# Stacked score matmuls, and PSUM banks taken by the planner's clocks

## The chip, the cores and the metric

The kernel runs on one core of a Trainium2 chip. The metric is the time of one execution on the device in microseconds (us). Three runs of the kernel before took 1472.0, 1473.97 and 1474.49 us; the median is 1473.97 us.

## The reference, cut to what matters

Two transformer-like blocks over 256 positions of width 1024, one after the other, all in float32. Four attentions lie in them, and the change is about their score matmuls:

```
# first block: an indexer picks 64 keys for each query, then 16 query heads over 4 key heads
logits = einsum('bqhd,bsd->bqhs', iqb, ik)            # 8 index heads of 64, one index key head
score  = einsum('bqhs,bqh->bqs', relu(logits), iwb)   # top 64 of it are the valid keys
att = einsum('bqgrd,bqkgd->bqgrk', qg, k_sel) * 64 ** -0.5   # 16 heads of 64, 4 key heads
p = softmax(where(valid, att, -inf)); o = einsum('bqgrk,bqkgd->bqgrd', p, v_sel)
# beside it in the first block: a gated recurrent layer (conv, two gates, scan) on 1024 channels
# second block, layer 0: differential attention, 4 heads with 2 maps of 64 each
sc = einsum('bqhmd,bshmd->bhmqs', q, k) * 64 ** -0.5; p = softmax(sc)
w = p[:, :, 0] - lam * p[:, :, 1]
# second block, layer 1: 8 query heads of 64 over 2 key heads, and beside it 8 heads of 96 (MLA)
```

Everything else is projections and five gated feed-forward layers (1024 to 2816 and back).

## The kernel before, in words

The 256 positions are two blocks of 128 rows. All big products (line 455) split each operand into a high and a low part and add three matmuls, `hi*hi`, `hi*lo`, `lo*hi`. Weights come in chunks of 128 x 1024 through six raw buffers; ScalarE copies a chunk to `WH` (line 403), VectorE subtracts to get `WL` (line 393), and TensorE runs through the chunks in order.

The program is written out by a planner in Python. Each engine has one queue in the order in which the planner emits, and a clock (`Q.at`) that an `Estimate` class advances by a guessed time for each instruction; `Q.when(token)` is the guessed end of an instruction. Big products are the main line. All else (attention units, the indexer called `chooser`, the recurrent steps `rnn`) are Python generators in a list `side`; `pump` steps those whose due time has come on TensorE's planned clock. In the fine stages a pump comes after every six matmuls of a 512-column product. Where the main line has to wait for a side branch, `onward` and `drain` step the branches alone and move TensorE's planned clock to the next due time.

PSUM has eight banks of 128 x 512 floats. `take` pops the bank that was given back longest ago; `give` puts a bank back with the token of its last reader. A taker emits its instruction at once, with a wait on that token: where the reader is late, TensorE stands in its queue and everything behind it stands too. `product` takes two banks, and before that steps branches until four are free.

An attention unit (function `one`, lines 576 to 679) handles two heads of one block of 128 queries. Its steps on TensorE: two transposes of a 128 x 64 query slice (line 586), copied to `QT` by ScalarE (line 587); two score matmuls (line 595), one for each head, whose weights are 64 x 128 (the head's 64 dimensions by 128 queries) and whose moving data are 64 x 128 or 64 x 256 of the turned keys `KT`; then softmax on VectorE and ScalarE (lines 609 to 625); transposes of the probabilities (line 650), copied to `PT` (line 654); products with the values (line 665), scaled into the output (line 671). Heads of 64 number 16 in the first block, 8 maps in layer 0 and 8 in layer 1, each for two query blocks, so 32 units have heads of 64; 8 units of MLA have heads of 96. Keys are turned by `turned_keys` (transposes at line 560, a ScalarE copy at line 563). The indexer does the same with 8 heads: transposes at line 1039, score matmuls at line 1052. A float32 matmul stands in the trace as two records, a transpose as one.

In layer 1 the keys of MLA are finished on VectorE (line 1583) before they are turned; layer 0 and layer 1 each end with a drained stretch, in which no product is left to cover the side branches.

Of the kernel before, what the change touches and what calls it, by code (L numbers as in the profile page):

```python
# [7 lines left out]
F32 = mybir.dt.float32  # L8
F32R = mybir.dt.float32r
# [49 lines left out]
class Estimate:  # L59
# [5 lines left out]
    def __init__(self):  # L65
        self.table = None

# [29 lines left out]
    def max(self, o, a):  # L97
        return 0.18 + 0.001 * width(a)
# [10 lines left out]
    def matmul(self, o, l, r, start=None, stop=None, skip_group_check=False):  # L109
        n = width(o)  # L110
        return max(0.108, 0.00045 * n) if l.dtype == F32R else max(0.215, 0.00177 * n)

    def transpose(self, o, i, ident):
        return 0.109
# [86 lines left out]
def build(nc, a, out):  # L201
    with ExitStack() as ctx:
        def sb(name, shape, dt=F32, c=ctx):
            return c.enter_context(nc.sbuf_tensor(name, shape, dt))
# [13 lines left out]
        SM = sb("SM", [128, 1024])  # L218
# [8 lines left out]
        with ExitStack() as c1:  # L227
# [14 lines left out]
            B1["T1"] = sb("T1a", [128, 320], F32, c1)  # L242
            B1["T2"] = sb("T1b", [128, 320], F32, c1)
        B2 = {}
        with ExitStack() as c1:
# [6 lines left out]
            B2["KT"] = sb("KT2", [128, 8, S], F32, c1)  # L252
# [8 lines left out]
        with ExitStack() as c1:  # L261
# [9 lines left out]
            B3["KG"] = sb("KG3", [128, 2, S], F32, c1)  # L271
# [21 lines left out]
        def program(plan):  # L293
# [7 lines left out]
            def small(n):  # L301
                i = pos["sm"]
                pos["sm"] += n
                assert pos["sm"] <= 1024
                return SM[:, i:i + n]
# [262 lines left out]

            def attention(units, d, dv, scale, PT, QT, slots, q, kt, v, kwaits, owaits, bias=None, lam=None, many=None, chosen=None, qs=None, sums=None, late=None, rings=None, first=0):
# [5 lines left out]
                def one(n, blk, hs, nk, o_ap):  # L575
# [4 lines left out]
                    qt = QT[0:d, n % nq, :]  # L580
# [63 lines left out]
                    held.add(("p", n % npt))  # L644
                    b, free = take()
# [12 lines left out]
                    while late is not None and not late:  # L658
                        yield
                    b, free = take()  # L660
# [220 lines left out]
            def rnn(p):  # L881
# [115 lines left out]
            IQT = B1["PT"][:, 0:2, :].rearrange("p a n -> p (a n)")  # L997
# [9 lines left out]
            def chooser():  # L1007
# [19 lines left out]
                ki = turned_keys(IKT, lambda b, h: QKI[:, b, 1792:1856], 1, 64, kr, bar)  # L1027
# [3 lines left out]
                for blk in range(2):  # L1031
                    yield
                    nk = 128 * (blk + 1)
                    kq = []
                    for h0 in (0, 4):
                        b, free = take()
                        for h in range(h0, h0 + 4):
                            j = (h - h0) * 128
                            tok = op("pe", lambda e, b=b, j=j, h=h, blk=blk: e.transpose(
                                PB[b][0:64, j:j + 128], heads[:, blk, 20 + h, :], ID[:, :]), free, kr)  # L1040
                        kq.append(op("act", lambda e, b=b, h0=h0: e.activation(
                            IQT[0:64, h0 * 128:h0 * 128 + 512], PB[b][0:64, :], ACT.Copy), tok, iq_free))
                        give(b, kq[-1])
                    kacc = None
                    for h in range(0, 8, 2):
# [29 lines left out]
                for h0 in (16, 0, 8):  # L1075
# [5 lines left out]
                kk = turned_keys(KT[:, :, :].rearrange("p h s -> p (h s)"),  # L1081
                                 lambda b, h: heads[:, b, 16 + h, :], 4, 64, kr2, bar)
# [4 lines left out]
                    units, 64, 64, 64 ** -0.5, B1["PT"], B1["QT"], [SR[:, i, :] for i in range(4)], lambda b, h: heads[:, b, h, :],  # L1087
                    lambda h: KT[:, h // 4, :], lambda kb, h: V1[:, kb, (h // 4) * 64:(h // 4) * 64 + 64],
# [161 lines left out]
            def layer0():  # L1250
# [5 lines left out]
                kws = Q.dma("pool", "d_ws", WS[:, :, :], a["ws"], bar)  # L1256
                rs_ = lambda: stage["rs"]
# [53 lines left out]
                def diff():  # L1311
                    while 0 not in turned_ or 1 not in turned_:
                        yield
                    yield turned_[1]
                    kk = turned_keys(KT[:, :, :].rearrange("p h s -> p (h s)"),
                                     lambda b, h: QK[:, b, 512 + h * 64:512 + h * 64 + 64], 8, 64, turned_[1], bar)
# [5 lines left out]
                        lambda b, h: QK[:, b, h * 64:h * 64 + 64], lambda h: KT[:, h, :],  # L1322
# [113 lines left out]
            def layer1():  # L1436
# [8 lines left out]
                gh = G[:, :, 0:640].rearrange("p b (h d) -> p b h d", d=64)  # L1445
# [29 lines left out]
                def gqa_heads(i, h0, h, name):  # L1475
# [8 lines left out]
                    ss, k = summed(SG[:, :, h0 * 64:(h0 + h) * 64], h, 64, kq)  # L1484
# [35 lines left out]
                def gqa():  # L1520
                    while "gk_n" not in flags:
                        yield
                    yield flags["gk_n"]
                    kk = turned_keys(KG[:, :, :].rearrange("p h s -> p (h s)"), lambda b, h: gh[:, b, 8 + h], 2, 64,
                                     flags["gk_n"], bar)
                    while "gq_n" not in flags:
# [7 lines left out]
                        units, 64, 64, None, B3["PT"], B3["QT"], rooms, lambda b, h: gh[:, b, h], lambda h: KG[:, h // 4, :],  # L1534
                        lambda kb, h: G[:, kb, 640 + (h // 4) * 64:640 + (h // 4) * 64 + 64],
# [86 lines left out]
                def evacuated(got_x, moves):  # L1622
# [8 lines left out]
                side.extend([gqa_heads(1, 8, 2, "gk"), gqa_heads(0, 0, 8, "gq"), gqa(), mla_shared(), mla_keys(),  # L1631
# [3 lines left out]
                    (lambda b: SG[:, b, 512:640], lambda p: p[:, 0:128], ACT.Square, rs_, rt_)))  # L1635
# [145 lines left out]
```

How the kernel before makes its waits and increments, by code:

```python
    def play(self, eng, e, sems):  # L173
        seen = {}
        for waits, fn, sem, n in self.q[eng]:
            need = {}
            for s, v in waits:
                if v > seen.get(s, 0):
                    need[s] = max(need.get(s, 0), v)
            for s, v in need.items():
                e.wait_ge(sems[s], v)
                seen[s] = v
            ins = fn(e)
            if n:
                ins.then_inc(sems[sem], n)
# [1508 lines left out]
        @block.sync  # L1694
        def _(e):
            Q.play("sp", e, sems)
            for s, v in final[0]:
                e.wait_ge(sems[s], v)
```

## Time and profile before

| what | value |
|---|---|
| median of three runs | 1473.97 us (1472.0 to 1474.49) |
| the profiled execution's own time | 1469.99 us |
| its span, first to last instruction | 1468.2 us |
| TensorE busy | 1418.3 us, 97% of the span, 7100 matmul records |
| VectorE busy | 881.9 us, 60% |
| ScalarE busy | 755.2 us, 51% |
| GpSimd busy | 10.6 us, 1% |
| DMA | 242.58 MB, 165 GB/s mean |
| mean granted TensorE clock | 0.986 of full speed |

The span ends at the last instruction; 1.8 us of the execution's time lie outside it. Busy shares are averages over stages: five feed-forward layers with nothing but big products, and three stages with attention in them (41 to 230 us, 698 to 772 us, 1172 to 1262 us). A matmul's record is longer than its share of the engine, because matmuls overlap: what one costs is read from the distance between starts.

### The profile page before, as it was taken

The page shows a single profiled execution, that of the slowest core. Times are in us where ns is not written, and L with a number is a line of the kernel's source. Part 1 is how long each engine was busy: PE and PEld are TensorE (multiplying, and loading weights), DVE is VectorE, ACT ScalarE, POOL GpSimd, SP SyncE. Part 2 cuts the span into 40 slices and gives each one's busy share as a digit, 9 for nine tenths or more (in the row PEclk, how much of TensorE's full clock was granted, in tenths as well). Part 3 has the DMA queues.
Part 4 walks back from the last instruction along what each step waited for, and adds up shares of the span by engine and source line. Part 5 has one row for each costly group of instructions (what it writes and reads, how often), then busy time and mean ns, then how long its engine had stood idle before and what let it go on. Part 6 is the DMA issues. An engine that isn't in the chain of part 4 may idle for free.

```text
span 1468.2 us, 18415 instructions
## 1 busy us (share of the span) xinstructions
PE 1418.3 (97%) x7100; PEld 1193.7 (81%) x7100; DVE 881.9 (60%) x1443; ACT 755.2 (51%) x1159; POOL 10.6 (1%) x18
## 2 busy tenths in 40 slices
PE   6999999899999999999979999999999979999999
PEld 6899887688887788888868888888888868888887
DVE  6878766655454645557876555555555684655553
ACT  5568754554443544445655544444444486554442
POOL 1000000000000000000000000000000000000000
PEclk9999999899999999999989999999999989999999
DMA  8544534465565465554525555655555440465561
GB/s 281 156 142 135 186 100 144 143 206 181 172 204 169 136 208 182 191 186 158 173 72 172 187 180 189 203 179 186 168 186 191 135 144 0 130 213 178 170 212 59
DMA packets 131768, 242.58 MB, mean 165 GB/s; under 512 B 8544, under 2 KB 21472, under 8 KB 131680
## 3 DMA queue, kind: packets, MB, share of 16 engines
q1 hardware_dynamic: 130768, 239.15, 50.7%
q0 software_dynamic: 624, 2.10, 0.5%
q8 instruction: 57, 0.93, 0.3%
q14 instruction: 31, 0.25, 0.1%
q10 hardware_dynamic: 288, 0.14, 0.0%
HBM read 240.31 MB, written 1.05 MB: 164 GB/s over the span
## 4 chain that ended last, share of the span: by engine, by line
PE 94%; DVE 3%; ACT 2%; DMA 0%; issue 0%; SPq 0%; DVEq 0%
PE PB L455 83%; PE PB L485 3%; PE PB L595 2%; PE PB L665 2%; PE PB L650 1%; PE PB L586 1%; PE PB L560 0%; PE PB L1052 0%; DMA X<-in_x_dram 0%; ACT SL L625 0%; DVE SM L530 0%; DVE SM L528 0%; DVE SM L529 0%; DVE WL L393 0%; PE PB L908 0%
## 5 line engine op out<-in xcount | busy, mean ns | idle before, releaser
L393 DVE TENSOR_TENSOR WL<-RAW,WH 128x1024 fp32r<-128x1024 f32 (+1 forms) x453 | 537.1, 1214 | 226.2 <-ACT WH L403 225.9
L403 ACT ACTIVATE WH<-RAW 128x1024 fp32r<-128x1024 f32 (+1 forms) x453 | 467.6, 1054 | 307.2 <-PE PB L455 304.2
L455 PE MATMUL PB<-WH,AT0h 128*128 128x512 f32 (+3 forms) x1328 | 505.0, 380 | 2.5 <-DVE AT0l L511 1.5
L455 PE MATMUL PB<-WH,AT0l 128*128 128x512 f32 (+3 forms) x1328 | 498.2, 375 | 0.0
L455 PE MATMUL PB<-WL,AT0h 128*128 128x512 f32 (+3 forms) x1328 | 498.2, 375 | 0.0
L455 PEld LDWEIGHTS PB<-WH,AT0h 128*128 128x128 f32 x1328 | 251.7, 190 | 47.3 <-ACT AT0h L506 2.2
L455 PEld LDWEIGHTS PB<-WH,AT0l 128*128 128x128 f32 x1328 | 251.3, 189 | 44.8
L455 PEld LDWEIGHTS PB<-WL,AT0h 128*128 128x128 f32 x1328 | 251.7, 190 | 42.2
L455 PE MATMUL PB<-WH,FTh 128*128 128x512 f32 x440 | 174.0, 395 | 0.0
L455 PE MATMUL PB<-WH,FTl 128*128 128x512 f32 x440 | 172.5, 392 | 0.0
L455 PE MATMUL PB<-WL,FTh 128*128 128x512 f32 x440 | 170.8, 388 | 0.0
L722 DVE SCALAR_TENSOR_TENSOR SR<-PB,SM,SR 128x512 f32<-128x512 f32 (+1 forms) x60 | 42.4, 706 | 136.0 <-PE PB L455 136.0
L455 PEld LDWEIGHTS PB<-WH,FTl 128*128 128x128 f32 x440 | 82.6, 188 | 19.3
L455 PEld LDWEIGHTS PB<-WL,FTh 128*128 128x128 f32 x440 | 82.6, 188 | 18.0
L455 PEld LDWEIGHTS PB<-WH,FTh 128*128 128x128 f32 x440 | 82.8, 188 | 16.0
L714 ACT ACTIVATE SR<-PB,SM 128x512 f32<-128x512 f32 (+1 forms) x60 | 39.3, 654 | 96.7 <-PE PB L455 93.8
L497 ACT ACTIVATE FTh<-PB 128x512 fp32r<-128x512 f32 x55 | 30.2, 596 | 103.2 <-PE PB L485 103.2
L500 DVE TENSOR_TENSOR FTl<-PB,FTh 128x512 fp32r<-128x512 f32 x55 | 35.7, 687 | 18.1 <-ACT FTh L497 18.1
L747 DVE SCALAR_TENSOR_TENSOR X<-PB,X 128x512 f32<-128x512 f32 x16 | 11.1, 692 | 49.6 <-PE PB L455 49.6
L455 PE MATMUL PB<-AT0h,WH 128*128 128x256 f32 x128 | 37.4, 292 | 0.0
L511 DVE SCALAR_TENSOR_TENSOR AT0l<-PB,CO,AT0h 128x256 fp32r<-128x256 f32 x64 | 26.7, 478 | 16.5 <-ACT AT0h L506 16.5
L455 PE MATMUL PB<-AT0l,WH 128*128 128x256 f32 x128 | 36.2, 283 | 0.0
(300 smaller groups left out, 1134.3 us busy)
## 6 DMA issues: line engine op xcount, KB each, us to landing
RAW<-in_ffn_w_gu_dram SPq DMA_DIRECT2D x88, 512.0 KB, 4.6
RAW<-in_ffn_w_gu_2b_dram SPq DMA_DIRECT2D x88, 512.0 KB, 4.5
RAW<-in_w_in_dram SPq DMA_DIRECT2D x48, 512.0 KB, 3.7
RAW<-in_ffn_w_down_dram SPq DMA_DIRECT2D x44, 512.0 KB, 4.2
RAW<-in_ffn_w_down_2b_dram SPq DMA_DIRECT2D x44, 512.0 KB, 4.1
RAW<-in_w_ffn_gate_dram SPq DMA_DIRECT2D x22, 512.0 KB, 4.5
RAW<-in_w_ffn_up_dram SPq DMA_DIRECT2D x22, 512.0 KB, 4.6
RAW<-in_w_ffn_down_dram SPq DMA_DIRECT2D x22, 512.0 KB, 4.6
```

The lines of the kernel that those rows point to most:

```text
L393: e.tensor_tensor(o, s, h, ALU.subtract), th, loaded[i], hl_free[i % NHL])
L403: th = op("act", lambda e, o=WH[i % NHL][:, 0:m], s=RAW[i % NRAW][:, 0:m]: e.activation(o, s, ACT.Copy), loaded[i], hl_free[i % NHL])
L455: e.matmul(o, l, r, start=s, stop=p, skip_group_check=feature_major)
L485: tok = op("pe", lambda e, o=o, s=src(blk, t): e.transpose(o, s, ID[:, :]), waits, free, ("d_id", 16))
L497: th = op("act", lambda e, o=hi, s=PB[b][:, 0:m]: e.activation(o, s, ACT.Copy), tok, dst.free)
L500: e.tensor_tensor(o, s, h, ALU.subtract), th, dst.free)
L511: e.scalar_tensor_tensor(o, s, g, h, ALU.mult, ALU.subtract),
L586: e.transpose(o, s, ID[:, :]), free, kwaits)
L595: e.matmul(o, qt[:, i * 128:i * 128 + 128], r, start=True, stop=True), tq, free, kwaits)
L665: e.matmul(o, pt[:, j:j + 128], r, start=kb == 0, stop=kb == nb - 1),
L714: tg = [op("act", lambda e, b=b, bank=bank, sl=sl, n=n, rs=rs: e.activation(sl[:, b, :], PB[bank][:, 0:n], ACT.Silu, scale=rs[:, b:b + 1]) ...
L722: k = dve(lambda e, b=b, bank=bank, sl=sl, n=n, rs=rs: e.scalar_tensor_tensor(sl[:, b, :], PB[bank][:, 0:n], rs[:, b:b + 1], sl[:, b, :], ...
```

## The change

Two heads' keys are laid into one buffer of 128 rows with zeros beside them (rows 0 to 63 by the columns of the first head, rows 64 to 127 by those of the second), so that one transpose of 128 x 128 queries and one matmul with 128 rows of weights and twice as many columns stands for two of each. `KT` and `IKT` grow for it and are zeroed by GpSimd; `stacked_keys` fills them. In layer 1 the weight columns are put in another order on the host, so that key heads lie where the pairs need them. MLA keeps its old form. The first block's query ring has four slots in place of two. `take` takes the bank whose last reader ends first by the planner's clocks; new `room` waits hold back an attention step or a recurrent step until a bank (or two) is free by TensorE's planned clock. `Estimate` adds 0.09 us where the count of weight rows goes over or under 64. After the keys of the first block are stacked, the branch waits for the copies before it starts attention. Cut to its core:

```diff
     def matmul(self, o, l, r, start=None, stop=None, skip_group_check=False):
         n = width(o)
-        return max(0.108, 0.00045 * n) if l.dtype == F32R else max(0.215, 0.00177 * n)
+        return self.turned(l.shape[0]) + (max(0.108, 0.00045 * n) if l.dtype == F32R else max(0.215, 0.00177 * n))
+    def turned(self, rows):
+        was, self.half = self.half, rows <= 64
+        return 0.09 if was != self.half else 0.0
...
-            B1["KT"] = sb("KT1", [128, 4, S], F32, c1)
-            B1["IKT"] = sb("IKT", [128, S], F32, c1)
+            B1["KT"] = sb("KT1", [128, 4, 2, S], F32, c1)
+            B1["IKT"] = sb("IKT", [128, 1, 2, S], F32, c1)
-            B1["QT"] = sb("QT1", [128, 2, S], F32, c1)
+            B1["QT"] = sb("QT1", [128, 4, 128], F32, c1)
...
             def take():
-                return banks.pop(0)
+                i = min(range(len(banks)), key=lambda i: Q.when(banks[i][1]))
+                return banks.pop(i)
+
+            def room(n=1):
+                while len(banks) < n or sorted(Q.when(t) for _, t in banks)[n - 1] > Q.at["pe"]:
+                    yield sorted(Q.when(t) for _, t in banks)[n - 1] if len(banks) >= n else None
...
+            def stacked_keys(dst, src, places, *waits):
+                toks = []
+                for p in range(0, len(places), 2):
+                    here = places[p:p + 2]
+                    b, free = take()
+                    for i in range(len(here)):
+                        for blk in range(2):
+                            s = src(blk, p + i)
+                            o = PB[b][0:s.shape[1], i * S + blk * 128:i * S + blk * 128 + 128]
+                            tok = op("pe", lambda e, o=o, s=s: e.transpose(o, s, ID[:, :]), waits, free, ("d_id", 16))
+                    for j in range(2):
+                        r = slice(64 * j, 64 * j + 64)
+                        use = [i for i, pair in enumerate(here) if pair[j] is not None]
+                        if use:
+                            k0, n = here[use[0]][j], len(use)
+                            k = op("act", lambda e, r=r, o=dst[r, k0:k0 + n, j, :],
+                                   s=PB[b][r, use[0] * S:(use[0] + n) * S].rearrange("p (i s) -> p i s", s=S):
+                                   e.activation(o, s, ACT.Copy), tok, waits)
+                            toks.append(k)
+                    give(b, k)
+                return toks
...
+                    yield from room()
                     b, free = take()
-                    for i, h in enumerate(hs):
-                        tok = op("pe", lambda e, o=PB[b][0:d, i * 128:i * 128 + 128], s=q(blk, h):
-                                 e.transpose(o, s, ID[:, :]), free, kwaits)
-                    tq = op("act", lambda e, s=PB[b][0:d, 0:256]: e.activation(qt, s, ACT.Copy), tok,
-                            qt_free[n % nq])
+                    if d == 64:
+                        tok = op("pe", lambda e, o=PB[b][:, 0:128], s=q(blk, hs[0]): e.transpose(o, s, ID[:, :]),
+                                 free, kwaits)
+                        tq = op("act", lambda e, s=PB[b][:, 0:128]: e.activation(qt, s, ACT.Copy), tok,
+                                qt_free[n % nq])
...
                     yield tq
+                    yield from room()
                     b, free = take()
...
-                    for i, h in enumerate(hs):
-                        tok = op("pe", lambda e, o=pv[:, i, :], i=i, r=kt(h)[0:d, 0:nk]:
-                                 e.matmul(o, qt[:, i * 128:i * 128 + 128], r, start=True,
-                                          stop=True), tq, free, kwaits)
+                    if d == 64:
+                        tok = op("pe", lambda e, r=kt(hs[0])[:, :, 0:nk]: e.matmul(pv, qt, r, start=True, stop=True),
+                                 tq, free, kwaits)
...
+                    yield from room()
                     b, free = take()
                     for i in maps:
                         for kb in range(nb):
...
+            kz1 = [op("pool", lambda e: e.memset(B1["IKT"][:, :, :, :], 0.0)),
+                   op("pool", lambda e: e.memset(B1["KT"][:, :, :, :], 0.0))]
-            one_ = small(128)
-            k1s = op("pool", lambda e: e.memset(one_, 1.0))
...
+                yield from room(2)
                 (br, fr), (bi, fi) = take(), take()
...
-                ki = turned_keys(IKT, lambda b, h: QKI[:, b, 1792:1856], 1, 64, kr, bar)
+                ki = stacked_keys(IKT, lambda b, i: QKI[:, b, (1728, 1792)[i]:1856], [(None, 0), (0, None)], kr, kz1)
...
-                        for i in range(2):
-                            j = (h + i) * 128
-                            tok = op("pe", lambda e, pv=pv, i=i, j=j, nk=nk: e.matmul(
-                                pv[:, i, :], IQT[0:64, j:j + 128], IKT[0:64, 0:nk], start=True, stop=True),
-                                free, kq, ki)
+                        tok = op("pe", lambda e, pv=pv, j=h * 64, nk=nk: e.matmul(
+                            pv, IQT[:, j:j + 128], IKT[:, 0, :, 0:nk], start=True, stop=True), free, kq, ki)
...
+                kk = stacked_keys(KT, lambda b, i: QKI[:, b, 960 + 64 * i:1088 + 64 * i],
+                                  [(None, 0), (0, 1), (1, 2), (2, 3), (3, None)], kr2, kqk, kz1)
+                yield kk
...
+                kz2 = op("pool", lambda e: e.memset(KT[:, :, :, :], 0.0), bar)
...
+                    kk = stacked_keys(KT, lambda b, i: QK[:, b, 512 + i * 128:640 + i * 128],
+                                      [(i, i) for i in range(4)], turned_[1], kz2)
...
+                kz3 = op("pool", lambda e: e.memset(KG[:, :, :, :], 0.0), bar)
...
+                    kk = stacked_keys(KG, lambda b, i: G[:, b, 512 + 64 * i:640 + 64 * i], [(None, 0), (0, 1), (1, None)],
+                                      flags["gk_n"], flags["gk"], kz3)
```

A `room` stands before each of the four bank takings of an attention unit (query transpose, scores, probability transposes, values), in MLA's units too.

## Rows read from the trace of the kernel before

**Rows 1.** The page: busy time and its share; the chain that ended last.
```profile
PE 1418.3 (97%) x7100; PEld 1193.7 (81%) x7100; DVE 881.9 (60%) x1443; ACT 755.2 (51%) x1159; POOL 10.6 (1%) x18
PE 94%; DVE 3%; ACT 2%; DMA 0%; issue 0%; SPq 0%; DVEq 0%
```
**Rows 2.** TensorE's waits: waiter, releaser, us in total, times, longest.
```profile
PE PB L650 <- ACT SR L625: 5.9, 2, 3.9
PE PB L665 <- DVE AT0l L1347: 0.9, 1, 0.9
PE PB L586 <- ACT KT L563: 0.7, 1, 0.7
```
**Rows 3.** Timeline of TensorE, layer 0: start, us, instruction, count.
```profile
713.35 0.39 PE L455 MATMUL PB<-WL,AT0h 128*128 128x512 f32 x1
713.58 0.40 PE L455 MATMUL PB<-WH,AT0l 128*128 128x512 f32 x1
713.91 1.13 PE L595 MATMUL PB<-KT,QT 64*128 64x256 f32 x4
714.97 0.50 PE L455 MATMUL PB<-WH,AT0h 128*128 128x512 f32 x1
715.30 0.39 PE L455 MATMUL PB<-WL,AT0h 128*128 128x512 f32 x1
```
**Rows 4.** The same view, first block: two score pairs in one visit.
```profile
188.22 0.39 PE L455 MATMUL PB<-WH,AT1l 128*128 128x512 f32 x1
188.54 1.99 PE L595 MATMUL PB<-KT,QT 64*128 64x256 f32 x8
190.46 0.51 PE L455 MATMUL PB<-WH,AT1h 128*128 128x512 f32 x1
```
**Rows 5.** The same view, first block: gate matmuls with 128 rows.
```profile
143.99 0.39 PE L455 MATMUL PB<-WH,AT0l 128*128 128x512 f32 x1
144.21 1.02 PE L905 MATMUL PB<-XC,GB 128*128 128x256 f32 x4
145.07 1.03 PE L908 MATMUL PB<-XC,GB 128*128 128x256 f32 x4
145.75 0.58 PE L455 MATMUL PB<-WH,AT0h 128*128 128x512 f32 x1
146.17 0.39 PE L455 MATMUL PB<-WL,AT0h 128*128 128x512 f32 x1
```
**Rows 6.** The same view: first and last of 29 visits of 64-row weights.
```profile
44.16 1.60 PE L1052 MATMUL PB<-IKT,PT 64*128 64x128 f32 x12
1238.62 1.13 PE L595 MATMUL PB<-KG,QT 64*128 64x256 f32 x4
```
**Rows 7.** The same view, first block: a pair of query transposes.
```profile
113.14 0.28 PE L455 MATMUL PB<-AT0h,WL 128*128 128x256 f32 x1
113.26 0.38 PE L586 MATMUL PB<-ID,QKI 128*64 128x128 f32 x2
113.39 0.36 PE L455 MATMUL PB<-AT0h,WH 128*128 128x256 f32 x1
113.59 0.28 PE L455 MATMUL PB<-AT0l,WH 128*128 128x256 f32 x1
```
**Rows 8.** Windows: busy us by engine (x instructions), granted clock, DMA share, GB/s.
```profile
160.00:180.00 20.00, 20.00 (x90) 16.18 (x90) 19.62 (x28) 13.96 (x19) 0.00 (x0) 1.00 0.59 195
1196.00:1203.00 7.00, 2.87 (x16) 1.88 (x15) 5.54 (x11) 6.97 (x16) 0.00 (x0) 0.94 0.63 201
1203.00:1213.00 10.00, 5.98 (x32) 5.80 (x32) 9.21 (x31) 7.97 (x17) 0.00 (x0) 0.53 0.05 20
1213.00:1250.00 37.00, 34.98 (x243) 30.08 (x240) 17.23 (x60) 26.06 (x81) 0.00 (x0) 1.00 0.00 0
```
**Rows 9.** Timelines of GpSimd and of VectorE, first stage.
```profile
0.74 1.81 POOL L817 MEMSET GB<- 128x2048 f32 x1 [0.29 <-POOLq L1771]
...
16.02 1.65 DVE L511 SCALAR_TENSOR_TENSOR AT0l<-PB,CO,AT0h 128x256 fp32r<-128x256 f32 x4
```

More of the change, by code:

```diff
@@ L66, in __init__ @@
         self.table = None
+        self.half = False
     def activation(self, o, i, func, bias=None, scale=None, accum_out=None):
@@ L110, in matmul @@
         n = width(o)
-        return max(0.108, 0.00045 * n) if l.dtype == F32R else max(0.215, 0.00177 * n)
+        return self.turned(l.shape[0]) + (max(0.108, 0.00045 * n) if l.dtype == F32R else max(0.215, 0.00177 * n))
     def transpose(self, o, i, ident):
-        return 0.109
+        return self.turned(i.shape[0]) + 0.109
+    def turned(self, rows):
+        was, self.half = self.half, rows <= 64
+        return 0.09 if was != self.half else 0.0
 class Queues:
@@ L303, in small @@
                 pos["sm"] += n
[L304 removed]
+                assert pos["sm"] <= 896
                 return SM[:, i:i + n]
@@ L587, in one @@
-                    tq = op("act", lambda e, s=PB[b][0:d, 0:256]: e.activation(qt, s, ACT.Copy), tok,
-                            qt_free[n % nq])
+                    if d == 64:
[3 more added lines that the diff above has]
+                                qt_free[n % nq])
+                    else:
+                        for i, h in enumerate(hs):
+                            tok = op("pe", lambda e, o=PB[b][0:d, i * 128:i * 128 + 128], s=q(blk, h):
+                                     e.transpose(o, s, ID[:, :]), free, kwaits)
+                        tq = op("act", lambda e, s=PB[b][0:d, 0:256]: e.activation(qt, s, ACT.Copy), tok,
+                                qt_free[n % nq])
@@ L589, in one @@
                     give(b, tq)
                     yield tq
+                    yield from room()
                     b, free = take()
                     pv = PB[b][:, :].rearrange("p (h k) -> p h k", h=2)[:, :, 0:nk]
-                    for i, h in enumerate(hs):
-                        tok = op("pe", lambda e, o=pv[:, i, :], i=i, r=kt(h)[0:d, 0:nk]:
-                                 e.matmul(o, qt[:, i * 128:i * 128 + 128], r, start=True,
-                                          stop=True), tq, free, kwaits)
+                    if d == 64:
+                        tok = op("pe", lambda e, r=kt(hs[0])[:, :, 0:nk]: e.matmul(pv, qt, r, start=True, stop=True),
+                                 tq, free, kwaits)
+                    else:
+                        for i, h in enumerate(hs):
+                            tok = op("pe", lambda e, o=pv[:, i, :], i=i, r=kt(h)[0:d, 0:nk]:
+                                     e.matmul(o, qt[:, i * 128:i * 128 + 128], r, start=True,
+                                              stop=True), tq, free, kwaits)
@@ L659, in one @@
                         yield
+                    yield from room()
                     b, free = take()
@@ L1033, in chooser @@
                     nk = 128 * (blk + 1)
[L1034 to L1043, printed above, removed]
+                    b, free = take()
+                    for j in range(4):
+                        tok = op("pe", lambda e, b=b, j=j, blk=blk: e.transpose(
+                            PB[b][:, j * 128:j * 128 + 128], QKI[:, blk, 1280 + j * 128:1280 + j * 128 + 128],
+                            ID[:, :]), free, kr)
+                    kq = op("act", lambda e, b=b: e.activation(IQT, PB[b][:, :], ACT.Copy), tok, iq_free)
+                    give(b, kq)
                     kacc = None
@@ L1086, in chooser @@
                 gen, done = attention(
-                    units, 64, 64, 64 ** -0.5, B1["PT"], B1["QT"], [SR[:, i, :] for i in range(4)], lambda b, h: heads[:, b, h, :],
-                    lambda h: KT[:, h // 4, :], lambda kb, h: V1[:, kb, (h // 4) * 64:(h // 4) * 64 + 64],
+                    units, 64, 64, 64 ** -0.5, B1["PT"], B1["QT"], [SR[:, i, :] for i in range(4)], lambda b, h: QKI[:, b, h * 64:h * 64 + 128],
+                    lambda h: KT[:, h // 4], lambda kb, h: V1[:, kb, (h // 4) * 64:(h // 4) * 64 + 64],
                     [kk, kr2, kqk, s_free, scored, bar], None,
@@ L1533, in gqa @@
                     gen, done = attention(
-                        units, 64, 64, None, B3["PT"], B3["QT"], rooms, lambda b, h: gh[:, b, h], lambda h: KG[:, h // 4, :],
-                        lambda kb, h: G[:, kb, 640 + (h // 4) * 64:640 + (h // 4) * 64 + 64],
+                        units, 64, 64, None, B3["PT"], B3["QT"], rooms, lambda b, h: G[:, b, h * 64:h * 64 + 128], lambda h: KG[:, h // 4],
+                        lambda kb, h: G[:, kb, (704, 512)[h // 4]:(768, 576)[h // 4]],
                         [kk, flags["gq_n"], flags["gk"][0], bar], flags["gq_n"], many=(4, 4.0), rings=rings,
```

31 lines of the change are left out of this document (13 added, 18 removed).

## The prediction

> **What bounds the kernel now.** I read the page first, then TensorE's waits, then its timeline around the instructions that the change touches. TensorE is busy for 97% of the span and 94% of the chain that ended last is TensorE's [rows 1]. So a TensorE instruction taken out is worth its distance between starts, as long as nothing else holds the place, and an instruction shortened on another engine is worth nothing by itself. TensorE's waits in the attention stages are few [rows 2]: 5.9 us for exponentials, 0.9 us for a bank that VectorE (line 1347) had not released, 0.7 us for the first block's turned keys. One place is different: in layer 1, from 1196 to 1213 us, TensorE works 2.87 of 7 and 5.98 of 10 us, while ScalarE (6.97 of 7) and then VectorE (9.21 of 10) are full [rows 8]. From 1213 to 1250 us no product is left, yet TensorE is again busy 34.98 of 37 us.
>
> **Score matmuls.** A pair with 64 rows stands alone between two products [rows 3]. The product's matmuls start 0.23 us apart, so the next was due at 713.58 + 0.23 = 713.81. It starts at 714.97, 1.16 us late, and its successor follows after 0.33 us in place of 0.23: the pair costs 1.26 us. Two pairs can stand together [rows 4]: due at 188.45, resumed at 190.46, 2.01 us, with the same 0.10 behind it 2.11. The second pair thus adds 0.85, and about 0.40 us is paid once for each visit, however many pairs it holds. Float32 matmuls with 128 rows are in the trace too [rows 5]: eight records of 256 columns, due at 144.22, resumed at 145.75 (1.53), the successor after 0.42 in place of 0.23 (0.19), together 1.72 us, 0.215 a record. Four such records would cost 0.86. A visit at 64 rows pays 1.26, one at 128 rows 0.86: 0.40 goes.
>
> The stacked matmul has 512 columns in two records. No float32 matmul with more than 256 columns is in the trace. I take columns in proportion, 2 x 0.43 = 0.86, the cost of four records there, since 256 columns are the nearest row. The ends: 0.40 saved a visit, or nothing if 0.40 belongs to this kind of matmul and not to its rows.
>
> The Trainium skill says, in "TensorEngine Tiling (Array Packing)", section "Key Properties", that a change of tiling mode drains the engine; the 0.40 agrees [rows 3, 4]. Against it, "TensorE: Matmul & The Clock Gate", section "Step-by-step: what each phase is for", says of the weight load that its time goes with columns and that the row count does not matter; by that the stacking itself would bring nothing, which is the second rival below.
>
> There are 29 visits (the first and the last are shown [rows 6]): 4 of the indexer, 13 of the first block's attention, 5 in layer 0, 7 in layer 1. The first two of layer 1 come before the full ScalarE and VectorE [rows 8] and will be waited away. 27 x 0.40 = 10.8 us.
>
> **Transposes.** A pair displaces the product from 113.26 to 113.39 [rows 7], and the successor comes after 0.20 in place of 0.12: 0.21 us, 0.105 each. A query transpose goes in each of 32 units, and 8 of the indexer's 16. Keys: the indexer has 2 more, the first block 2 more, layer 0 8 fewer, layer 1 2 more, in all 2 fewer. Less the two units of layer 1 before its full stretch, 40 x 0.105 = 4.2 us. A transpose of 128 columns of weights in place of 64 I take at the same price; the 128-column transposes at line 485 or 650 are the same kind of instruction, and if it cost double, the whole 4.2 would go.
>
> **Waits.** The new wait behind the stacked keys lets products fill the 0.7 us of line 586 [rows 2]; nothing is queued behind it, since a branch that yields emits nothing. The bank wait at line 1347 (0.9) I count as nothing: it lies in layer 0's drained end, where later waits decide. `room` puts no wait on an engine; it delays the emitting. I take it at nothing, because late banks cost TensorE about 0.9 us in all before, so the planner rarely has cause to hold a step back. What it costs otherwise is the first rival.
>
> **ScalarE and GpSimd.** Query copies have half the columns, the stacked keys need more copies (five for two in the first block, three for one in layer 1); TensorE's products hide both. Layer 1's lie before 1196 us. GpSimd zeroes 512 + 2048 + 2048 + 1024 floats a partition; by 1.81 us for 2048 [rows 9] that is 5.0 us, on a queue that is 1% busy. The first two come beside VectorE's `AT0l` at 16 us [rows 9], which gates the first products. If VectorE stood still meanwhile, 2.3 us would be lost there and 5.0 in all; I take nothing and keep 5.0 as the end.
>
> **What comes back.** The first block's TensorE work shrinks against a VectorE that is at 19.62 of 20 us from 160 to 180 us [rows 8]; there TensorE can get no faster for long. Up to 187 us, 13 visits and 16 transposes go (5.2 + 1.7 = 6.9 us). The stretch is 14% of the 146 us from 41 to 187 us, 1.0 us; since faster products draw VectorE's work together elsewhere too, I take twice that, 2.0 us back. The ends are nothing and all 6.9.
>
> **The sum.** 10.8 + 4.2 + 0.7 - 2.0 = 13.7 us. The profiled execution took 1469.99 us, so 1456.3. The median of the runs shown is 3.98 above it: 1460.3 us.
>
> **Rivals.**
> First, slower: `room` starves the attention. A step held back waits for the next pump, six product matmuls or 6 x 0.23 = 1.38 us later. Layers 0 and 1 have 24 units with four such points, about four units in flight: if each point were held once, 24 x 4 x 1.38 / 4 = 33 us of attention would slide into drained stretches that nothing covers. At half of them it is 16.6, and the time is 1473.97 - 13.7 + 16.6 = 1477 us. It decides from about four points in ten. For it: layer 1 has 37 us without a product [rows 8]. Against it: TensorE is busy for 95% of them, so banks came in time, and there the planned clock jumps to the next due time without a pump.
> Second, only the transposes pay: the 0.40 stays with the stacked matmul. Then 4.2 + 0.7 less 0.5 (29% of the 1.7) is 4.4 us: 1469.6. For it: the stacked form is in no row. Against it: the gate matmuls are float32 too, between the same products, and lack the 0.40 [rows 5].
> Third, the new order takes away layer 1's stall: of 17 us from 1196 to 1213, TensorE idles 8.2, and from 1203 to 1213 its granted clock is 0.53, near the lower of its two levels (1.2 GHz), after it had stood. If the wait for the exponentials (3.9) and half of the 4.7 lost to the clock go, 6.3 more: 1454. Against it: the full engines there are ScalarE and VectorE, whose work hardly changes.
> Fourth, the planner's new order, not `room`, loses what TensorE gains, by VectorE's queue in the first block and the ends of the layers, 13.7 back: 1474, no change.
>
> **How the numbers follow.** Forecast 0.60, first rival 0.11, second 0.13, third 0.08, fourth 0.08. About 0.2% (2.9 us) can be told from no change. Faster: 0.60 + 0.13 + 0.08 = 0.81; same 0.08; slower 0.11. The range goes from 1453 (the third rival) to 1471 (the second, with 1 us of GpSimd's 5.0); it leaves out the first and the fourth.
>
> **What would show it.** Right: line 595 with 128 x 128 weights and 512 columns, two records, displacing the product by about 0.86 us; no visit with 64 rows left; one transpose in each unit of heads of 64; the first block and layer 0 each shorter by their share (about 9 and 4 us); feed-forward stretches unchanged. Wrong: a displacement near 1.26 (second rival); TensorE idle between 1213 and 1250 us or at the end of layer 0, while banks stand free (first); TensorE waiting for `WL` between 120 and 190 us for more than 2 us (the sum's last term).

## The result, and the profile after

The changed kernel took 1457.18 us (median of four runs, 1455.81 to 1459.47) against 1473.32 us for the kernel before (four runs, 1472.0 to 1474.49): a ratio of 0.989, 95% interval 0.9875 to 0.9904. The forecast was 1460.3. The profiled execution took 1455.81 us and its span fell from 1468.2 to 1454.0 us.

The page of the changed kernel: busy time and its share for each engine, then the chain that ended last, which answer to [rows 1].

```profile
PE 1403.6 (97%) x6978; PEld 1178.1 (81%) x6978; DVE 881.2 (61%) x1443; ACT 752.4 (52%) x1163; POOL 14.2 (1%) x21
PE 93%; DVE 3%; ACT 3%; DMA 0%; issue 0%; SPq 0%; DVEq 0%
```

TensorE lost 14.7 us of busy time and the span 14.2. That near equality doesn't yet say where. For that I cut the span at the first of the transposes of `X`, which stand in every kernel at the ends of the stages. Timelines of TensorE around these transposes, before:

```profile
282.06 0.47 PE L485 MATMUL PB<-ID,X 128*128 128x128 f32 x1 [5.39 <-DVE X L778]
...
672.71 0.38 PE L485 MATMUL PB<-ID,X 128*128 128x128 f32 x2
777.89 0.38 PE L485 MATMUL PB<-ID,X 128*128 128x128 f32 x2
1159.15 0.49 PE L485 MATMUL PB<-ID,X 128*128 128x128 f32 x3
1273.03 0.49 PE L485 MATMUL PB<-ID,X 128*128 128x128 f32 x3
```

and after:

```profile
276.97 0.47 PE L495 MATMUL PB<-ID,X 128*128 128x128 f32 x1 [5.40 <-DVE X L825]
...
668.44 0.38 PE L495 MATMUL PB<-ID,X 128*128 128x128 f32 x2
770.93 0.49 PE L495 MATMUL PB<-ID,X 128*128 128x128 f32 x3
1152.18 0.38 PE L495 MATMUL PB<-ID,X 128*128 128x128 f32 x2
1258.88 0.38 PE L495 MATMUL PB<-ID,X 128*128 128x128 f32 x2
```

With one more cut, at the first transpose of the indexer's keys (41.59 us before, 41.88 after), the differences of these starts give the length of each stage. The table has them for all kernels that ran, each in its profiled execution, as us more or less than before; the two feed-forward stretches not listed stayed within 0.4 us.

| kernel | run time, median | start | first block | feed-forward after it | layer 0 | layer 1 |
|---|---|---|---|---|---|---|
| changed | 1457.18 | +0.3 | -5.4 | +0.8 | -2.7 | -7.2 |
| e1 stacking alone | 1461.45 | +4.0 | -4.5 | +0.5 | -2.4 | -7.1 |
| e2 stacking, `room` | 1460.24 | +4.0 | -5.4 | +1.4 | -2.7 | -7.1 |
| e3 stacking, `take` | 1459.54 | +4.3 | -4.5 | +0.8 | -2.4 | -7.2 |
| e4 `room`, `take` alone | 1477.59 | +3.8 | +1.6 | +0.9 | +1.2 | -0.3 |
| e5 two matmuls, 128 rows | 1459.35 | +0.2 | -5.2 | +0.7 | -2.7 | -7.2 |
| e6 first of them 64 rows | 1472.76 | +4.6 | +3.5 | +0.3 | +0.2 | -5.8 |
| e7 query transposes twice | 1470.54 | +4.8 | +2.1 | +1.2 | +0.8 | -7.0 |
| e8 zeroing twice | 1458.46 | +3.9 | -5.4 | +1.4 | -2.7 | -7.3 |
| e9 as e7, order kept | 1461.45 | +3.9 | -4.1 | +0.2 | -2.5 | -7.0 |
| e10 even column cut | 1452.63 | -2.4 | -5.4 | +1.1 | -2.7 | -7.3 |
| e11 TensorE kept at work | 1455.75 | +4.7 | -5.4 | -1.6 | -4.7 | -6.8 |
| e12 e10 and e11 together | 1448.25 | -2.1 | -5.4 | -2.0 | -4.7 | -6.8 |

The start is told of last; it has two lengths, some 4 us apart, so stages are compared without it. The run times of one kernel fall into groups about as far apart (the changed kernel's are 1455.81 and 1455.85, 1458.51 and 1459.47). The feed-forward behind the first block varies with how long the granted clock stood at its lower level there (15.5 us before, 17.0 in e9, 18.5 in e2 and e8), so differences of up to 1 us in that column aren't put down to a part of the change. The kernel before took 1473.1, 1474.2 and 1474.0 us beside e1 to e4, e5 to e8 and e9 to e12.

### The profile page after: what moved, and what is told of

It reads as the page before. It is cut to its first block, busy times and chain, and to the rows that moved or that the text cites. A ratio compares the mean times of both kernels' runs of the same rounds, so it can differ in the third digit from the quotient of the medians.

```text
span 1454.0 us, 18198 instructions
## 1 busy us (share of the span) xinstructions
PE 1403.6 (97%) x6978; PEld 1178.1 (81%) x6978; DVE 881.2 (61%) x1443; ACT 752.4 (52%) x1163; POOL 14.2 (1%) x21
## 4 chain that ended last, share of the span: by engine, by line
PE 93%; DVE 3%; ACT 3%; DMA 0%; issue 0%; SPq 0%; DVEq 0%
PE PB L465 84%; PE PB L495 3%; PE PB L712 2%; PE PB L635 1%; PE PB L696 1%; PE PB L640 0%; DMA X<-in_x_dram 0%; PE PB L1095 0%; ACT WH L413 0%; DVE SM L540 0%; DVE SM L538 0%; DVE SM L539 0%; DVE WL L403 0%; ACT SR L670 0%; PE PB L953 0%
```

## The experiments

My theory was that stacking pays through the rows of the score weights and through the transposes, while banks and zeroing cost nothing. The rival was that the new order of the work or the bank rule carries the gain.

**e1 to e4: the parts apart.** Stacking with the old `take` and without `room` (e1), with `room` (e2), with the new `take` (e3), and the bank rule put into the kernel before (e4):

```diff
             def take():
-                i = min(range(len(banks)), key=lambda i: Q.when(banks[i][1]))
-                return banks.pop(i)
+                return banks.pop(0)          # e1, e2
             def room(n=1):
-                while len(banks) < n or ...
+                return                       # e1, e3
+                yield
```

> The changed kernel with the old bank rule (the bank given back longest ago) and no room waits: stacking alone. Theory (the gain is TensorE instructions and visits of 64-row weights that are gone): 12 to 18 us below the kernel before, so 1455 to 1462 us, within 3 us of the changed kernel. Rival (the planner's new bank rule and waits carry a good part of the gain): at most 10 us below, 1463 us or more.

> Stacking and the room waits, with the old bank rule. Theory: within 3 us of stacking alone, since late banks cost TensorE under 1 us before. Rival (room starves the attention): 4 us or more slower than stacking alone, and TensorE idle in the first block at the recurrent steps' end (the changed kernel has 3.5 us of stalls between 171 and 179 us there) or at the ends of layers 0 and 1.

> Stacking and the new bank rule, without room waits. Theory: within 3 us of stacking alone. Rival (room starves the attention): 2 us or more faster than the changed kernel, and the stalls of 3.5 us between 171 and 179 us gone.

> The kernel before with the new bank rule and the room waits, and no stacking. Theory: within 3 us of the kernel before, 1470 to 1477 us. Rival (the planner carries part of the gain): 5 us or more below it, 1468 us or less. Rival (room starves): 3 us or more above it.

Ratios to the kernel before: e1 0.992 (0.9904 to 0.9936), e2 0.9906 (0.9889 to 0.9923), e3 0.9902 (0.9885 to 0.992), e4 1.0029 (1.0016 to 1.0042). Stacking alone brings most of the gain: over the stages without the start, 13.5 of the changed kernel's 14.5 us. (Its median lies 4.3 us above the changed kernel's, more than the 3 expected; 3.7 of them are the start.) Among the three stacked kernels the intervals overlap; only the stages tell them apart, and barely: `room` takes 0.9 us off the first block (e2 against e1), which the feed-forward behind gives back in e2, though not in the changed kernel (against e3); `take` does nothing (e3 against e1). Without stacking the same bank rule makes the kernel slower, by 4.4 us by the medians and 3.4 over the stages (1.6 in the first block, 1.2 in layer 0). That lies outside the theory's 3 us and where the rival, that `room` starves the attention, had put it; which of the two parts costs it was not tried apart.

**e5 and e6: rows or instructions.** e5 issues each stacked matmul, the indexer's too, as two of half the columns, still with 128 rows; e6 gives the first of the two 64 rows. In e6 the price of a change of rows is also taken out of the planner.

```diff
-                        tok = op("pe", lambda e, r=kt(hs[0])[:, :, 0:nk]: e.matmul(pv, qt, r, ...
+                        for i in range(2):
+                            d_ = 128                 # e6: 64 + 64 * i
+                            tok = op("pe", lambda e, i=i, d_=d_, r=kt(hs[0])[0:d_, i, 0:nk]: e.matmul(
+                                pv[:, i, :], qt[0:d_, :], r, ...
```

> The changed kernel with each stacked score matmul split into two of half the columns, both with all 128 rows of weights (the zeros stay). Theory (what goes is the price of 64-row weights, once a visit): the pair still costs about 0.86 us at 256 columns, so within 2 us of the changed kernel, about 1457 to 1460 us. Rival (the gain comes from having one instruction for two, or from 512 columns): up to 40 x 0.40 = 16 us slower than the changed kernel, and 5 us at least.

> The same split into two, but the first of the two has only the upper 64 rows of weights and keys (the zeros below are left out), so that visits of 64-row weights are back, one for each of the 40 pairs; columns and instructions are those of the split kernel, and the planner's added 0.09 us is taken out so that it writes the same order. Theory: 40 x 0.40 = 16 us, less some that waits hide, so 11 to 16 us slower than the split kernel. Rival (by the rule that rows do not matter): within 2 us of the split kernel.

e5 0.9901 (0.9883 to 0.9918), e6 0.9994 (0.9983 to 1.0004): 13.4 us between them. One pair of the changed kernel, between products whose starts are 0.23 us apart (timeline of TensorE, first block):

```profile
212.76 0.39 PE L465 MATMUL PB<-WH,AT1l 128*128 128x512 f32 x1
212.99 1.02 PE L635 MATMUL PB<-KT,QT 128*128 128x512 f32 x2
213.44 0.79 PE L465 MATMUL PB<-WH,AT1h 128*128 128x512 f32 x1
214.08 0.39 PE L465 MATMUL PB<-WL,AT1h 128*128 128x512 f32 x1
```

The product was due at 212.99 and came 0.45 later, its successor after 0.64 in place of 0.23: 0.86 us. The same pair in e5:

```profile
212.87 0.40 PE L465 MATMUL PB<-WH,AT1l 128*128 128x512 f32 x1
213.10 1.02 PE L636 MATMUL PB<-KT,QT 128*128 128x256 f32 x4
213.77 0.58 PE L465 MATMUL PB<-WH,AT1h 128*128 128x512 f32 x1
214.20 0.40 PE L465 MATMUL PB<-WL,AT1h 128*128 128x512 f32 x1
```

0.67 + 0.20 = 0.87 us with twice the instructions. And a pair of e6, layer 0:

```profile
718.15 0.39 PE L465 MATMUL PB<-WH,AT0l 128*128 128x512 f32 x1
718.47 1.32 PE L637 MATMUL PB<-KT,QT 64*128 64x256 f32 x4
719.45 0.58 PE L465 MATMUL PB<-WH,AT0h 128*128 128x512 f32 x1
719.87 0.40 PE L465 MATMUL PB<-WL,AT0h 128*128 128x512 f32 x1
```

Due at 718.38, resumed 1.07 later, the successor 0.19 late: 1.26 us, as in [rows 3]. One group of 64 rows in the pair is enough to bring back the whole 0.40. (The group of four records carries the shape of its first.) Where the time goes shows in TensorE's weight loads (PEld), e6 and then e5:

```profile
718.47 0.29 PEld L637 LDWEIGHTS PB<-KT,QT 64*128 64x128 f32 x2 [0.35 <-issue]
719.10 0.30 PEld L637 LDWEIGHTS PB<-KT,QT 128*128 128x128 f32 x2 [0.33 <-issue]
```

```profile
212.87 0.85 PEld L636 LDWEIGHTS PB<-KT,QT 128*128 128x128 f32 x4
```

In e5 one load follows another without a break. In e6 no load runs for 0.35 us before the weights of 64 rows and for 0.33 before the weights of 128 rows behind them. The 40 visits of e6 cost 8.7 us in the first block, 2.9 in layer 0 and 1.4 in layer 1, in all 13.0, or 0.33 each.

**e7 and e9: the transposes.** Both issue each of the 32 query transposes a second time; in e9 the planner prices the second one at nothing, so that it writes the order of the changed kernel.

```diff
+                        for x in range(2):
+                            tok = op("pe", lambda e, ..., x=x: 0.0 if x and isinstance(e, Estimate)
+                                     else e.transpose(o, s, ID[:, :]), free, kwaits)   # e7: without the 0.0
```

> The changed kernel with each of the 32 stacked query transposes issued twice into the same place. Theory: 32 x 0.105 = 3.4 us slower than the changed kernel, less the few that waits hide: 2 to 4 us. Rival (transposes are hidden, or one of 128 columns costs double): under 1 us, or 6 us and more.

> The changed kernel with each of its 32 query transposes issued twice, as in the run before that did so, but with the second one at no price in the planner, so that the order of the work stays that of the changed kernel. Theory A (the planner's other order made that run some 12 us slower, the transposes themselves 0.105 us each): 32 x 0.105 = 3.4 us slower than the changed kernel, range 2 to 4.5, and no second half-clock stretch in the first block. Theory B (the transposes themselves are that dear, by the queues behind them): again about 12 us slower.

e7 0.9972 (0.9958 to 0.9987): 11 to 12 us slower than e5 and e8 beside it, outside the 2 to 4 that I expected and, by its size alone, in the rival's range. e9 0.9914 (0.9901 to 0.9928): 4.3 us above the changed kernel by the medians, 3.6 of them the start. So most of e7's loss was the order that the planner wrote when it counted 0.1 us more for a unit, and the rival's reason, a transpose at double price, does not hold. Windows of the end of the first block show it (busy us by engine with instructions, granted clock, DMA share, GB/s), e7:

```profile
225.00:241.00 16.00, 11.92 (x46) 9.95 (x47) 6.86 (x11) 6.90 (x12) 0.00 (x0) 0.68 0.11 34
```

and e9:

```profile
225.00:241.00 16.00, 14.93 (x77) 12.43 (x77) 9.89 (x13) 7.13 (x9) 0.00 (x0) 1.00 0.48 165
```

In e7 the last units of attention slid behind the products; TensorE waited 2.6 us there for an exponential, and the granted clock then stood at the lower level. In e9 the doubled transposes cost 1.3 us in the first block and 0.2 in each of layers 0 and 1, 1.7 in all: 0.05 us each. The granted clock fell elsewhere in e9 (it stood at the lower level for 6.8 us of layer 0 in place of 10.2, and for 10.2 of layer 1 in place of 6.8), so this is an estimate.

**e8: the zeroing.** Each buffer is zeroed twice on GpSimd, one after the other.

```diff
-            kz1 = [op("pool", lambda e: e.memset(B1["IKT"][:, :, :, :], 0.0)), ...
+            kz1 = None
+            for _ in range(2):
+                kz1 = [op("pool", lambda e: e.memset(B1["IKT"][:, :, :, :], 0.0), kz1), ...
```

> The changed kernel with GpSimd's four zeroings done twice. Theory (nobody waits for them): within 1 us of the changed kernel. Rival (VectorE stands still meanwhile): 2 us slower from the first two alone, up to 5 us, with VectorE's AT0l near 16 us or its neighbours lengthened by 2 us.

0.9896 (0.9879 to 0.9914), and no stage differs from e2 by more than 0.2 us: the zeroing costs nothing.

**e10 to e12: what the traces pointed to.** e10 cuts 584 columns of the first block's input product as 296 + 288 in place of 512 + 72. e11 puts matmuls of no use (result unread, no price in the planner) where TensorE stands: five before each of the two waits for `X` (277 and 474 us in the changed kernel), two and four at the end of layer 0, four before layer 1's wait for the exponentials. e12 does both.

```diff
-            for b, (bank, tok) in enumerate(product("w_in", 3584, 512, at0, 8)):
+            for b, (bank, tok) in enumerate(product("w_in", 3584, 296, at0, 8)):    # e10
...
-            for b, (bank, tok) in enumerate(product("w_in", 4096, 72, at0, 8)):
+            for b, (bank, tok) in enumerate(product("w_in", 3880, 288, at0, 8)):
...
+            def warm(n):                                                            # e11
+                b, free = take()
+                for _ in range(n):
+                    tok = op("pe", lambda e, b=b: 0.0 if isinstance(e, Estimate) else e.matmul(
+                        PB[b][:, :], ID[:, :], row("sgu"), start=True, stop=True), free, ...)
+                give(b, tok)
```

> The changed kernel with the first block's last two products cut as 296 + 288 columns in place of 512 + 72 (ScalarE copies the index query and key columns of both, VectorE scales the 8 weights); the output is the same. A matmul of the 72-column product takes 0.112 us of TensorE's line and one of 512 columns 0.227, together 0.339. Theory A (time goes by columns down to about 256 and not below half of it: 2 x 0.135 = 0.27): 48 x 0.07 = 3.3 us less on TensorE, and the half-clock stretch at 29 to 36 us, which costs some 3.5 us where an execution has it, is gone, since it falls in the 72-column product: 3 to 6.5 us faster than the changed kernel. Theory B (time goes by columns plus a fixed part per matmul, the same for each, and the clock falls by what comes earlier): no gain beyond 0.5 us and the stretch stays.

> The changed kernel with matmuls of no use (identity by a row table, 512 float32 columns, 0.86 us each) put where TensorE idles for others before its clock falls: 5 at the first block's X waits near 470 us, 2 and 4 at layer 0's end near 750 us, 4 in layer 1 before the wait for the exponentials near 1195 us; the planner prices them at nothing, and the output is the same. Theory A (the granted clock falls because TensorE stood, and the stretch behind costs half of its length): the half-clock stretches at 472 and 756 us (10.24 each, in the changed kernel) and at 1196 us (6.83) go, 3 to 5 us of matmul time each, 6 to 12 us faster than the changed kernel, less 1 to 3 us where a matmul of no use delays one of use. Theory B (what follows the waits is bound by ScalarE and VectorE, and the slow clock lies under it): within 2 us of the changed kernel, though the stretches go. Theory C (the clock falls all the same): 1 to 4 us slower.

> The even cut of the first block's last two products and the matmuls of no use at TensorE's waits together. If both effects hold and add: 3 to 6.5 us and 3 to 9 us less than the changed kernel, 1441 to 1451 us. If the kept clock is hidden anyway: 1451 to 1455. If neither does anything: 1457 to 1460.

e10 0.9855 (0.9842 to 0.9869), e11 0.9878 (0.9865 to 0.9892), e12 0.9825 (0.9812 to 0.9839). e12, at 1448.25 us, beats both kernels; its interval lies clear of the change's 0.9875 to 0.9904. e10's gain is all in the start, 2.7 us shorter than in the changed kernel. Starts of its 288-column matmuls:

```profile
27.89 0.29 PE L465 MATMUL PB<-WH,AT0h 128*128 128x288 f32 x1
28.02 0.29 PE L465 MATMUL PB<-WL,AT0h 128*128 128x288 f32 x1
```

They are 0.13 us apart, those with 72 columns 0.11 (last section): a quarter of the columns for over four fifths of the time. That was Theory A.

e11 against the changed kernel is unclear by the medians, since the start cost it more in its profile; e12 against e10, on one chip, is 4.4 us. The stages: 3.1 us less in the feed-forward behind the first block, 2.0 in layer 0, 0.5 lost in layer 1. Timelines at the end of the first block's feed-forward, changed kernel:

```profile
474.15 1.97 PE L495 MATMUL PB<-ID,X 128*128 128x128 f32 x8 [5.40 <-DVE X L825]
```

and e12:

```profile
465.00 4.45 PE L564 MATMUL PB<-RW,ID 128*128 128x512 f32 x10
470.56 1.09 PE L495 MATMUL PB<-ID,X 128*128 128x128 f32 x8 [1.11 <-DVE X L832]
```

The eight transposes take 1.97 us after TensorE stood for 5.40, and 1.09 us after it stood for 1.11. Windows of the 11 to 12 us behind, changed kernel:

```profile
474.00:486.00 12.00, 11.11 (x41) 9.11 (x42) 8.31 (x26) 8.84 (x19) 0.00 (x0) 0.65 0.17 45
```

and e12:

```profile
470.50:482.00 11.50, 9.06 (x46) 7.33 (x47) 7.97 (x26) 9.46 (x20) 0.00 (x0) 1.00 0.15 46
```

The clock stays at its upper level (1.00 against 0.65), yet each of the two places gives back some 1.5 us, not the 3 to 5 expected: with the clock up, TensorE stands for 2.44 of 11.5 us, waiting for the turned inputs. Theory A held for the mechanism, Theory B for much of the size. Layer 1's stretch stayed in spite of four matmuls; there TensorE still stood 3.4 us for an exponential, and what comes next there waits for VectorE in every kernel (told of below, under layer 1), so nothing was to be gained ahead of it.

## Why the prediction was right, point by point

**Score matmuls.** Right, price and cause. 0.86 us for a stacked pair was read off the gate matmuls and came out as 0.86; 29 visits became none. e5 and e6 put the 0.40 on the rows and not on the count of instructions. The Trainium skill's drain at a change of tiling mode ("TensorEngine Tiling (Array Packing)", section "Key Properties") agrees with that (1.26 us in e6 against 0.87 in e5), if going from 128 rows to 64 is such a change, which no row names. The Trainium skill's sentence that the row count does not matter ("TensorE: Matmul & The Clock Gate", section "Step-by-step: what each phase is for") is about the time of a weight load, and there it agrees with the trace: loads of 64 rows took 0.18 to 0.19 us before, and so did loads of 128. It says nothing of the gaps between loads, where the visits pay; the prediction's second rival read too much into it.

**Transposes.** The distance between starts was right, the worth too large. A lone transpose of the changed kernel moves its successors by 0.12 us (159.40 for a due 159.37, then 0.32 in place of 0.23):

```profile
159.14 0.39 PE L465 MATMUL PB<-WH,AT0l 128*128 128x512 f32 x1
159.37 0.27 PE L619 MATMUL PB<-ID,QKI 128*128 128x128 f32 x1
159.40 0.49 PE L465 MATMUL PB<-WH,AT0h 128*128 128x512 f32 x1
159.72 0.40 PE L465 MATMUL PB<-WL,AT0h 128*128 128x512 f32 x1
```

But e9 gives 0.05 us for each one added; if one taken out is worth the same, the term of 4.2 was about 2.1. Why the rest was not worth its distance between starts no run shows; TensorE waiting anyway in some of the stretches is a guess.

**What comes back.** The size about held (TensorE stands 2.6 us longer, as shown below, against 2.0), the cause did not. I had named VectorE's `WL` as the engine that the first block would meet. TensorE's waits in the changed kernel from 165 to 185 us name ScalarE alone:

```profile
PE PB L635 <- ACT QT L621: 1.1, 2, 0.9
PE PB L712 <- ACT PT L700: 0.9, 2, 0.5
PE PB L696 <- ACT SR L658: 0.8, 1, 0.8
```

Windows of these 20 us, before:

```profile
165.00:185.00 20.00, 19.75 (x94) 15.85 (x93) 15.93 (x26) 12.91 (x22) 0.00 (x0) 1.00 0.57 185
```

and after:

```profile
165.00:185.00 20.00, 17.18 (x88) 13.45 (x87) 16.19 (x37) 12.06 (x38) 1.38 (x2) 1.00 0.43 131
```

TensorE stands for 2.8 us in place of 0.25 with neither VectorE nor ScalarE full. Each wait is that of one step of a unit for the step just before it (a query copy, a probability copy, an exponential), with few products between them: from 171.7 to 176.8 us the timeline has none. It isn't `room` that makes them: from 165 to 195 us TensorE stands for 2.9 us in e1 and e3, which lack it, as against 2.8 in the changed kernel and 0.25 before. That shorter steps on TensorE cover these hand-overs less is my reading; no run tried it.

**The stages.** By its terms the forecast had the first block 7.6 us shorter (17 visits, 20 transposes, the keys' 0.7, less 2.0), layer 0 3.7 (5 visits, 16 transposes) and layer 1 2.4 (5 and 4). Measured: 5.4, 2.7 and 7.2, and 0.8 longer in the feed-forward. The first two are short, I take it, by the transposes' smaller worth and the hand-overs; layer 1 is where the term was mis-sized, by 4.8 us, and the two errors cancel. The first block's other sign in the prediction, about 9 us shorter, did not come either. So the sum (13.7 us, for a span that fell by 14.2) was better than its parts, and that was luck. Its last step was no constant: the median lay 3.98 us above the profiled execution before and 1.37 after, which is 2.6 of the 3.1 us between forecast and median.

**Layer 1.** Of the third rival's two parts the clock's came (some 3.4 us) and the wait's did not. Among TensorE's waits from 1159 to 1273 us stands, before, beside the exponentials of [rows 2]:

```profile
PE PB L560 <- DVE K L1583: 4.3, 1, 4.3
```

and from 1152 to 1259 us, after:

```profile
PE PB L696 <- ACT SR L670: 8.1, 3, 3.8
```

The wait of MLA's key transposes for VectorE (4.3 us) is gone, but a second wait for exponentials (3.7 us) stands in its place, and nothing was won by that. The transposes themselves, before:

```profile
1207.02 3.65 PE L560 MATMUL PB<-ID,K 128*96 128x128 f32 x16 [4.29 <-DVE K L1583]
```

and after, with VectorE's last step on the keys ahead of them:

```profile
1199.03 1.22 DVE L1628 TENSOR_TENSOR K<-K,SM 128x1024 f32<-128x1024 f32 x1
1200.53 2.98 PE L570 MATMUL PB<-ID,K 128*96 128x128 f32 x16
```

They start 47.9 us into the stage before and 48.3 after, both times within 0.3 us of VectorE's last step on `K`; in all fourteen profiles it is 47.8 to 48.6 us. So the stage up to them is as long as these keys take on VectorE, whatever TensorE saves there, and the whole gain lies behind them. Windows from the transposes to the end of the stage, before and after:

```profile
1207.02:1273.03 66.01, 63.74 (x383) 55.26 (x384) 33.90 (x92) 41.12 (x105) 0.00 (x0) 0.93 0.16 48
```

```profile
1200.53:1258.88 58.35, 57.47 (x360) 49.28 (x359) 33.52 (x91) 40.06 (x103) 0.00 (x0) 0.98 0.17 55
```

Behind them the stage lost 7.7 us: 1.4 of standing (66.01 - 63.74 = 2.27, 58.35 - 57.47 = 0.88) and 6.3 of busy time. Of the busy time 2.4 are the visits and transposes as forecast, if they are worth their full price. Some 3.4 go with the clock: 0.07 of 66 us was lost at the lower level before and 0.02 of 58 after, 4.6 against 1.2 us. The last 0.5 I can't assign. So what the sum had at nothing here is the clock and the standing behind the keys. This does not hang on the visits: e6, with its 64-row groups back, keeps 5.8 of the 7.2, and e4, with the bank rule alone, has none of it and still waits 4.5 us for `K`. So stacking brings it. Which part of stacking does (fewer transposes of a unit, the keys' copies, the new place of the key heads, or the order that the planner then writes), and why the clock came back sooner, was not tried alone and stays open.

**Waits and rivals.** The 0.7 us of the keys' copies is gone from the waits. `room`, counted as nothing, was worth between nothing and 0.9 us (e2 against e1). The first rival did not come: in the stretch without products TensorE is busy for 36.44 of 37 us, so banks came in time (window of layer 1, after):

```profile
1209.00:1246.00 37.00, 36.44 (x260) 32.65 (x261) 18.60 (x59) 29.83 (x86) 0.00 (x0) 1.00 0.05 15
```

The prediction's other sign of it, TensorE idle at the end of layer 0, doesn't point to `room`: in layer 0 TensorE stands for 8.6 us in the changed kernel, 8.1 before, and 10.0 in e1, which has no `room`. The second rival is refuted by the displacement of 0.86. The fourth, that an order of the planner loses what TensorE gains, did not come here, but e7 shows that it was near: 0.1 us in the planner's price of a unit moved the time by some 9 us (e7 against e9). The 0.08 looks low for it.

## What to carry to other kernels

Read the price of a small matmul as what it does to its neighbours' starts, and count visits, not instructions: half-height weights between full-height ones cost 0.40 us a visit here, and zeros that fill the height cost less than that. Where a planner writes the order, a part of a change can only be tried with the order held (price it at nothing), or the run measures the order. Narrow slices of a product are worth evening out first, and where TensorE stands for several microseconds, the granted clock behind the wait is part of the wait's price: matmuls of no use put there were worth 1.5 to 2 us at each of three places, and lost some 0.5 at the fourth, where the next work waited for VectorE anyway. A wait that is gone from the list is not yet time won: find the next point that another engine fixes, and see whether that came sooner.

## What the runs showed of the hardware that was not expected

The start of the kernel has two lengths, some 4 us apart, though TensorE, once it has begun at 11 us, waits in neither. Windows of the changed kernel and of e3:

```profile
29.00:36.00 7.00, 7.00 (x42) 6.09 (x42) 4.41 (x19) 2.13 (x2) 0.00 (x0) 1.00 0.45 143
```

```profile
29.00:36.00 7.00, 7.00 (x33) 6.42 (x33) 2.70 (x10) 1.18 (x2) 0.00 (x0) 0.58 0.21 73
```

In e3 the granted clock falls to the lower of its two levels (1.2 GHz) at about 30 us, in the middle of matmuls of 72 columns whose records leave no gap; their starts are 0.11 us apart until then and 0.20 to 0.22 behind it:

```profile
29.93 0.29 PE L465 MATMUL PB<-WH,AT0l 128*128 128x72 f32 x1
30.04 0.40 PE L465 MATMUL PB<-WH,AT0h 128*128 128x72 f32 x1
30.24 0.41 PE L465 MATMUL PB<-WL,AT0h 128*128 128x72 f32 x1
```

So the clock fell here while TensorE had no wait. Nine of the fourteen profiles have this fall, at 29 to 31 us, and they are the nine with the long start; among the five without it are both kernels with the even cut. That is one profile for each of e10 and e12, and the run times settle no more: those of e12, without the 72 columns, lie within 0.8 us and the changed kernel's within 3.7, but e9's, with the 72 columns, within 1.6. What makes the clock fall here is not shown.
